# Attention stage of a two-layer streaming encoder: a written order for each engine, first scores among the latent queries, first output halves made in the last tile

## The chip, the cores and the metric

The kernel runs on one core of a Trainium2 chip. The metric is the device time of one execution in microseconds, the median over runs. An execution takes in both layers and both kinds of requests.

## What is computed

Two layers of an encoder run on 1024 prompt tokens and on 8 samples of 16 tokens (1152 tokens, 9 tiles of 128, or 3 blocks of 384). Cut to what matters:

```python
h = rmsnorm(x, norm_g) * (1.0 + scale[:, None]) + shift[:, None]     # shift, scale, gate = silu(c) @ w_mod + b_mod
z = h @ w_in                                # split into conv, latent-attention, local-attention parts
cq = rmsnorm(m_q, q_norm_g); qm = cq @ w_uq # 4 heads: 128 without, 64 with rotary position
kv = ckv_all @ w_ukv                        # keys and values from a latent of 128
s = (einsum(q_nope, k_nope) + einsum(q_rope, k_rope)) * MLA_SCALE    # chunk-causal mask, chunks of 64
p = softmax(s); o_mla = einsum(p, v)        # samples also attend to a cache of 512 keys each
out = concatenate([out_conv, out_mla, out_swa]) @ w_out
x = x + gate[:, None] * out                 # after the second layer a final rmsnorm
```

Everything is float32. Large products are made of three products of float32r parts: hi x hi, lo x hi and hi x lo, where hi is a value rounded on ScalarE and lo is the rest, subtracted on VectorE.

## The kernel before

Each engine has an instruction stream of its own, executed in order; semaphores tie them together. A layer is: the input projection in 22 column chunks, with the local attention tiles spread between the last of them; the latent attention stage; the output projection (`first_out`, `out_a`, `out_b`, lines 997 to 1033). The change concerns the middle part and its two edges.

**Queries.** TensorE makes six rope products (`q_rope`, line 1184, banks 0 to 3) and twelve latent products (`q_latent`, line 1193, a head's weights folded with the key weights, banks 4 to 7), each of 384 columns. ScalarE rotates a rope product by four copies (`turn_query`, line 1530) and copies the even latent ones (`latent_query`, line 1535); VectorE finishes the ropes (`rope_query`, line 1957) and copies the odd latent ones (line 1963). In the old order all of them come before the first scores: scores wait for every rope (`roped`) and every latent copy (`all_latent_queries`, line 1216).

**Groups, jobs, units.** `plan_attention` (line 104) lays out 12 groups: prompt tiles in the order 2, 0, 1, 3, 4, 5, 6, 7 and four pairs of samples between the later ones. A prompt tile has 4 score jobs (one a head, 36 jobs with the samples') and one unit for each key tile (44 units). A job goes: `scores` on TensorE into a bank, or two from tile 4 on (`banks_of`); `maxima` on VectorE (line 1990); `exps` on ScalarE (line 1548); `normalise` on VectorE (line 1996). A unit goes: `turn_probs` on TensorE (line 1268, transposes into bank 4 or 5), a copy to SBUF (even units ScalarE, line 1613, odd ones VectorE), `weigh` on TensorE (line 1287, accumulates in bank 6). After a group: `out` on ScalarE (line 1556), `up_values` on TensorE (line 1310, bank 7), `gate_mla` on VectorE (line 2002), which leaves a tile of `mix`, the input of the output projection. From tile 3 on scores are made of hi and lo parts: `split_keys` (line 1573) once, `split_q` (line 1580) and `stack_q` (line 1592) for each tile, on ScalarE and VectorE.

**Other work in the stage.** Four rows of this layer's gate modulation and, in the first layer, eight of the next layer's are computed from w_mod (`modulation`, line 949, bank 7; copied by VectorE; turned by TensorE, L1346; copied again). SyncE loads w_mod rows, sample caches and w_out blocks of 256 columns into two slots of `raw`, in an order sorted by where the steps stand (`when`, `todo`).

**The order.** `plan_steps` (line 174) writes one list for all engines by rules: scores up to a group ahead, each unit turned one ahead of its weighing. Each engine walks the same list, `STEPS`, and does its own share of each step:

```python
for j in range(GROUPS[1]["jobs"][-1] + 1):
    scores()
    exps(j)
    norms(j - 1)
```

**The edge to the output projection.** After the list, ScalarE makes six pieces of `h_hi` (three blocks by two halves of the 8 rows, line 1630) and VectorE six of `h_lo` (`lo`, line 1763; the last tile's gate between the first and the second). Then both split w_out columns 2 to 5 (ScalarE L1441, VectorE L1811). TensorE's `first_out` makes column blocks 0 and 1 for token blocks 0 and 1, half by half, and `out_a(2)` follows once `residual_a(0)` (line 2066) has read the first. The splits of w_out columns 0 and 1 stand in the last tile, behind the turnings of its units 4 and 6 of 8. SyncE loads the residual `x` (two transfers of 2.3 MB) once the first piece of `h_hi` is made (line 753 to 755). `probs` has 9 slots; `slot_of` (line 143) gives a tile's four jobs slots (2, 3, 6, 7) or (4, 5, 0, 1) in turn; slots 0 to 5 share memory with `h_hi`.

Of the kernel before, what the change touches and what calls it, by code (L numbers as in the profile page):

```python
# [103 lines left out]
def plan_attention():  # L104
# [28 lines left out]
MOD_AT = {(0, 1): 0, (2, 1): 1, (3, 1): 2, (3, 3): 3, (5, 1): 4, (5, 3): 5, (7, 1): 6, (7, 3): 7, (7, 5): 8,  # L133
          (9, 1): 9, (9, 3): 10, (9, 5): 11}
INDEX = {key: gi for gi, key in enumerate(ORDER)}
SPLIT_AT = {1: 3, 2: 4, INDEX["s", 0]: 5, INDEX["s", 1]: 6, INDEX["s", 2]: 7}
NEXT_P = {gi: min((i for i in range(gi + 1, len(ORDER)) if ORDER[i][0] == "p"), default=None) for gi in range(len(ORDER))}
# [36 lines left out]
def plan_steps():  # L174

    steps, done, row = [], {"exp": -1, "norm": -1, "turn": -1, "scores": -1}, None

    def put(what, i):
        steps.append((what, i))
        if what in done:
            done[what] = i

    def exps(upto):
        while done["exp"] < min(upto, done["scores"]):
            j = done["exp"] + 1  # L190
            if SLOT_FREE[j] is not None and SLOT_FREE[j] > done["turn"]:
                return
            put("exp", j)

    def norms(upto):
        while done["norm"] < min(upto, done["exp"]):
            put("norm", done["norm"] + 1)

    def stack(t):
        if ("stack_q", t) not in steps:  # L200
            put("stack_q", t)

    def scores():
        g = GROUP_OF[done["scores"] + 1]
        if g["kind"] == "mla_p" and g["idx"] >= SPLIT_FROM:
            stack(g["idx"])
        put("scores", done["scores"] + 1)
        put("maxima", done["scores"])

    def may_score():  # L210
        j = done["scores"] + 1
        return j < NJOBS and (BANKS_FREE[j] is None or BANKS_FREE[j] <= done["exp"])

    def turn(n):
        if done["turn"] < n:
            put("turn", n)
            put("copy", n)

    for j in range(GROUPS[1]["jobs"][-1] + 1):
        scores()  # L220
        exps(j)
        norms(j - 1)
    norms(GROUPS[0]["jobs"][-1])
    for gi, g in enumerate(GROUPS):
        units = g["units"]
        to = NEXT_P[gi]
        ahead = NJOBS - 1 if to in (None, LAST) else GROUPS[to]["jobs"][-1] + (ORDER[to + 1][0] == "p")
        js = range(done["scores"] + 1, ahead + 1)
        at = [max(len(units) - 1, 1) * i // len(js) for i in range(len(js))]
        if gi in SPLIT_AT:  # L230
            put("split_q", SPLIT_AT[gi])
        if gi == 2:
            put("samples", 0)
        for q, n in enumerate(units):
            for _ in range(at.count(q)):
                exps(done["scores"])
                if may_score():
                    scores()
            if (gi, q) in MOD_AT:
                put("mod", MOD_AT[gi, q])  # L240
                row = MOD_AT[gi, q]
            turn(n)
            if (gi, q) == (0, 1):
                put("split_keys", 0)
            if n < units[-1]:
                turn(n + 1)
            elif gi < LAST and done["exp"] >= GROUPS[gi + 1]["jobs"][-1]:
                norms(GROUPS[gi + 1]["jobs"][-1])
                turn(n + 1)
            if q == 0 and gi - 1 in UP_OF:  # L250
                put("up", gi - 1)
            put("weigh", n)
            if n == units[-1]:
                put("out", gi)
            if q == 0 and gi in SPLIT_AT:
                stack(SPLIT_AT[gi])
            if row is not None and ((gi, q) not in MOD_AT or n == units[-1]):
                put("modT", row)
                row = None
            before = done["exp"]  # L260
            exps(done["scores"])
            norms(before)
            if gi == LAST and q in (3, 5):
                put("split", NIN + q // 4)
        while done["scores"] < ahead:
            exps(done["scores"])
            assert may_score()
            scores()
        if gi < LAST:
            exps(GROUPS[gi + 1]["jobs"][-1])  # L270
            norms(GROUPS[gi + 1]["jobs"][-1])
    return steps


STEPS = plan_steps()
# [30 lines left out]
def build(nc, io):  # L306
# [61 lines left out]
    probs_s = at("probs_s", SPL_AT + 12288, [P, 640])  # L368
# [231 lines left out]

    def p_view(j):
        return probs(j)[:, 0:job_width(j)]

    local_s = psum[:, 6:8, 0:2 * P]
    local_t = psum[:, 6:8, 2 * P:4 * P]
    local_v = psum[:, 6, 2 * P:4 * P]

    with nc.Block() as block:
# [235 lines left out]
        def _(pe):  # L844
# [100 lines left out]
            def layer(L, last):  # L945
# [51 lines left out]
                def first_out():  # L997
# [3 lines left out]
                    for n in range(2):  # L1001
                        for half in range(2):
                            pe.wait_ge(lo_h.sem, lo_h.at(lane.layer, 2 + 2 * n + half + 1))
                            for s in range(2):
                                mm = products(s, [(n, 3 * s + n)], HALF_K[half])
                                if n == 1 and half == 1:
                                    mm.then_inc(z_done.sem, 1)
# [1212 lines left out]
```

## Time and profile before

| | |
|---|---|
| median of 3 runs | 1353.84 us (1346.69 to 1364.53) |
| the profiled execution | 1350.68 us, its span 1348.9 us |
| mean granted TensorE clock | 0.952 |
| TensorE busy | 1249.6 us (93%) |
| VectorE busy | 612.6 us (45%) |
| ScalarE busy | 415.0 us (31%) |
| GpSimd busy | 63.2 us (5%) |
| first layer: first query product, steady output products | 373.45 us, 611.25 us |
| second layer: the same | 1020.6 us, 1241.83 us |

Times in rows are microseconds from the start of the span. PE is TensorE (PEld its weight loads), DVE VectorE, ACT ScalarE, POOL GpSimd, SP SyncE. PEclk is the clock that was granted to TensorE: 1.00 is 2.4 GHz, 0.50 is 1.2 GHz. In a view of stretches a line gives start and end, length, then the busy time (and number of instructions) of PE, PEld, DVE, ACT and POOL, PEclk, the DMA share and GB/s. A wait is idle time of an engine, put down to the work whose end released it.

### The profile page before, as it was taken

What the parts mean: (1) busy time and instruction counts of PE and PEld (TensorE: products, weight loads), DVE (VectorE), ACT (ScalarE), POOL (GpSimd) and SP (SyncE); (2) the same over time, 40 slices, a digit from 0 to 9 for tenths busy, and PEclk for the clock granted to TensorE, in tenths of its full rate; (3) what the DMA queues carried; (4) which work ended last, traced back from release to release, by engine and by line L of the source; (5) the groups of instructions that cost most, each with busy time, mean ns of one, the idle gap of its engine ahead of it and who ended that gap; (6) DMA issues with size and microseconds to landing.
All of it is one profiled execution on the core that took longest, in us unless ns stands there. A gap on an engine that the chain in (4) does not pass through costs nothing.

```text
span 1348.9 us, 18240 instructions
## 1 busy us (share of the span) xinstructions
PE 1249.6 (93%) x7420; PEld 1086.0 (81%) x7420; DVE 612.6 (45%) x1064; ACT 415.0 (31%) x775; POOL 63.2 (5%) x51
## 2 busy tenths in 40 slices
PE   5699999999998899989989999899999889998997
PEld 4599998999955556669989999899996456667996
DVE  3852313346265555553285232233635545555134
ACT  5432311222254234342143232122224334434111
POOL 1100010000000000002120001000000000000211
PEclk9799988999997789999999998999999889998998
DMA  9821211110241135245121112111022203106002
GB/s 349 306 67 31 62 45 32 32 32 28 93 138 42 41 124 164 95 172 181 41 85 55 62 34 73 32 32 32 28 68 99 106 32 102 39 1 240 10 32 110
DMA packets 72063, 112.98 MB, mean 84 GB/s; under 512 B 3617, under 2 KB 55977, under 8 KB 70706
## 3 DMA queue, kind: packets, MB, share of 16 engines
q1 hardware_dynamic: 71986, 111.92, 24.4%
q8 instruction: 52, 0.85, 0.3%
q14 instruction: 25, 0.20, 0.0%
HBM read 94.44 MB, written 16.42 MB: 82 GB/s over the span
## 4 chain that ended last, share of the span: by engine, by line
PE 82%; DVE 10%; ACT 4%; issue 2%; DMA 1%; SPq 1%; DVEq 0%; POOLq 0%; POOL 0%; ACTq 0%
PE psum L964 52%; PE psum L1250 5%; PE psum L1305 4%; PE psum L1284 3%; PE psum L1199 2%; DVE h_lo L1766 2%; DVE h_lo L1775 1%; PE psum L1301 1%; DVE w_lo L1811 1%; PE psum L1190 1%; DMA modw<-in_w_mod 1%; PE psum L955 1%; PE psum L1259 1%; PE psum L1262 1%; DVE scaled L1751 1%
## 5 line engine op out<-in xcount | busy, mean ns | idle before, releaser
L964 PE MATMUL psum<-h_hi,w_hi 128*128 128x384 f32 x1440 | 493.1, 342 | 16.6 <-DVE h_lo L1766 9.5
L964 PE MATMUL psum<-h_lo,w_hi 128*128 128x384 f32 x1440 | 486.3, 338 | 0.0
L964 PE MATMUL psum<-h_hi,w_lo 128*128 128x384 f32 x1440 | 486.0, 337 | 0.0
L964 PEld LDWEIGHTS psum<-h_hi,w_hi 128*128 128x128 f32 x1440 | 274.3, 191 | 23.8 <-issue 18.7
L964 PEld LDWEIGHTS psum<-h_hi,w_lo 128*128 128x128 f32 x1440 | 274.5, 191 | 0.0
L964 PEld LDWEIGHTS psum<-h_lo,w_hi 128*128 128x128 f32 x1440 | 273.9, 190 | 0.0
L1811 DVE TENSOR_TENSOR w_lo<-raw,w_hi 128x1024 fp32r<-128x1024 f32 x62 | 77.1, 1244 | 264.8 <-ACT w_hi L1441 264.3
L1441 ACT ACTIVATE w_hi<-raw 128x1024 fp32r<-128x1024 f32 x62 | 65.7, 1060 | 297.7 <-PE psum L964 216.2
L1993 DVE TENSOR_REDUCE smax<-psum 128x1 f32<-128x640 f32 (+7 forms) x72 | 55.1, 765 | 91.3 <-PE psum L1251 60.7
L1305 PE MATMUL psum<-pT,ckv 128*128 128x512 f32 x144 | 79.2, 634 | 3.3 <-DVE pT L1814 3.3
L1497 ACT ACTIVATE probs_p<-psum,nmax 128x128 f32<-128x128 f32 (+1 forms) x72 | 25.2, 362 | 138.2 <-DVE esink L1811 138.2
L804 POOL TENSOR_TENSOR sq_a<-sq_a,sq_a 128x768 f32<-128x768 f32 x12 | 22.1, 1842 | 894.6 <-ACT sq_a L1395 894.6
L1446 ACT ACTIVATE rot<-psum 32x384 f32<-32x384 f32 (+1 forms) x80 | 59.2, 740 | 8.5 <-DVE svT L1812 5.7
L1553 ACT ACTIVATE probs_lo<-psum,nmax 128x128 f32<-128x128 f32 (+7 forms) x48 | 36.1, 751 | 68.5 <-issue 36.2
L1812 DVE SCALAR_TENSOR_TENSOR x<-psum,mod,x 128x768 f32<-128x768 f32 (+1 forms) x32 | 24.0, 751 | 68.7 <-PE psum L964 67.9
L1613 ACT ACTIVATE pT<-psum 128x512 f32<-128x512 f32 (+1 forms) x44 | 25.0, 568 | 90.8 <-PE psum L1284 47.2
L1812 DVE SCALAR_TENSOR_TENSOR mix<-psum,mix 64x256 f32<-64x256 f32 (+1 forms) x54 | 27.6, 512 | 48.5 <-PE psum L1098 21.1
L1284 PE MATMUL psum<-ident,probs_lo 128*128 128x128 f32 x220 | 40.9, 298 | 8.8 <-DVE probs_hi L1813 5.8
L1284 PEld LDWEIGHTS psum<-ident,probs_lo 128*128 128x128 f32 x220 | 26.1, 149 | 24.9 <-issue 23.5
L1250 PE MATMUL psum<-ckv_hi,qa_hi 128*128 128x512 f32 x72 | 38.6, 537 | 6.3 <-ACT qst L1596 6.3
L1395 ACT ACTIVATE sq_a<-x 128x768 f32<-128x768 f32 x16 | 13.5, 847 | 88.1 <-DVE x L1812 88.1
L1814 DVE COPY pT<-psum 128x512 f32<-128x512 f32 (+1 forms) x44 | 28.8, 655 | 12.9 <-PE psum L1284 10.5
(216 smaller groups left out, 1421.5 us busy)
## 6 DMA issues: line engine op xcount, KB each, us to landing
raw<-in_w_in SPq DMA_DIRECT2D x18, 1024.0 KB, 5.2
raw<-in_w_mod SPq DMA_DIRECT2D x15, 1024.0 KB, 5.1
x<-xT_scratch SPq DMA_DIRECT2D x4, 2304.0 KB, 12.0
modw<-in_w_mod SPq DMA_DIRECT2D x8, 1024.0 KB, 15.0
raw<-in_w_out SPq DMA_DIRECT2D x10, 768.0 KB, 5.4
tab<-in_c_rope SPq DMA_DIRECT2D x6, 1152.0 KB, 5.9
tok<-in_x_prompt SPq DMA_DIRECT2D x2, 2048.0 KB, 10.2
ckvT_c<-in_cache_mla_ckvT SPq DMA_DIRECT2D x8, 512.0 KB, 3.6
```

Of the source, the lines that this page charges most:

```text
L964: mm = pe.matmul(psum[:, bank, 0:BLK], w_[:, k, :], h[:, k, blk(n)], start=(k == 0 and i == 0), stop=(k == KD - 1 and i == 2))
L1199: mm = pe.matmul(psum[:, 4 + m % 4, 0:BLK], mq[:, k, h, :], cq[:, k, blk(n)], start=(k == 0), stop=(k == 1))
L1250: pe.matmul(out[:, a:b], q, k[:, a:b], start=(n == 0), stop=(n == 4 and b < w))
L1284: mm = pe.transpose(out[:, tile(h)], probs(g["jobs"][h])[:, tile(i)], ident[:])
L1305: mm = pe.matmul(psum[:, 6, :], ckv[:, g["keys"][i], :], pT[:, n % 3, :], start=(i == 0), stop=last_one)
L1441: lane.link(act.activation(view(w_hi[w_slot(c)]), src, ACT.Copy), hi_w)
L1446: ins = act.activation(pick(rot[a:a + 32, :]), src[b:b + 32], ACT.Copy)
L1553: lane.link(act.activation(p_view(j), s_view(j), ACT.Exp, bias=nmax[:, s, 0:1], scale=MLA_SCALE, accum_out=psum_p[:, s, 0:1]), expd)
L1811: tt = lambda *a, sig=None: lane.link(dve.tensor_tensor(*a), sig)
L1812: stt = lambda *a, sig=None: lane.link(dve.scalar_tensor_tensor(*a), sig)
L1814: cp = lambda *a, sig=None: lane.link(dve.tensor_copy(*a), sig)
L1993: lane.link(dve.tensor_reduce(smax[:, s, 0:1], s_view(j), AX.X, ALU.max))
```

## The change

1. `plan_steps` and `STEPS` go. Three strings, one for TensorE, ScalarE and VectorE each, give each engine its own order; a letter is a kind of step, and steps of one kind keep their numbers' order. The query products, their rotations and copies are now steps too.
2. TensorE's order begins with ropes 0 to 3 and latents 0 to 6; then scores alternate with the rest: s0, latent 7, s1, rope 4, s2, rope 5, s3, latent 8, s4, latent 9, s5, latent 10, s6, latent 11, s7. Scores need only the latent copies of block 0 and ropes 0 to 3. Ropes 4 and 5 move from banks 0 and 1 into the ring of banks 4 to 7 (`RING`).
3. The split of the keys is two steps; krT's comes first, among the rotations. Query tile 3 is split after the first exponential. The hi and lo keys' and `probs_s`'s places are shifted to allow it.
4. w_mod rows, sample scores, gates and splits stand elsewhere in the stage; in TensorE's order the second w_mod row comes before unit 3 and the value products of groups later by one to five units.
5. The first two pieces of `h_hi` and `h_lo` are halves (block 0, rows 0 to 3) and (block 1, rows 0 to 3); ScalarE and VectorE make them, and the splits of w_out columns 0 and 1, within the last tile: the first half and both splits between the copies of units 34 to 39, the second half at the very end. `slot_of` now gives tiles slots 0 to 3 or 4 to 7, so that the first half's place is free. `first_out` takes the halves in the order of `OUT_HALVES`.
6. SyncE's waits follow: the first sample cache still waits for all latent products, w_mod and w_out loads are sorted by the new places, and `x` is loaded once the last latent output is copied (`ol_c`) and all value products but the last are made.

```diff
@@ def slot_of(j):
     if g["kind"] == "mla_p":
-        return ((2, 3, 6, 7), (4, 5, 0, 1))[side(g["idx"])][i]
+        return HEADS * side(g["idx"]) + i
...
-STEPS = plan_steps()
+RING = [("latent", m) for m in range(2 * HEADS)] + [("rope", 4), ("rope", 5)] + [("latent", m) for m in range(2 * HEADS, 3 * HEADS)]
+OUT_HALVES = ((0, 0), (1, 0), (0, 1), (1, 1), (2, 0), (2, 1))
...
+LETTERS = dict(r="rope", l="latent", s="scores", x="maxima", e="exp", n="norm", t="turn", c="copy", w="weigh", o="out", u="up",
+               m="mod", f="modT", k="keys", q="query", z="stack", b="samples", v="weights", h="half")
+TENSOR_ORDER = (
+    "rrrrlllllllslsrsrslslslslsssstmtwtwfsssmtwstwfsstuwtwmtwfsmtwsstuwtwsstwstuwstuwstwfstwmtwfstwmtwfsm"
+    "twstwfsmtwtwtwftwtuwssmtwstwfstwmtwftwtwsstwtwmtwftuwtwmtwtwtwtwtuwtwftwuw")
+SCALAR_ORDER = (
+    "rrrlrlklleqererelzekelqeeceeceeeoecoeqecozecezeeocqezeceoeceqcezoceeoceeccoeceoecececehocvcvocccho")
+VECTOR_ORDER = (
+    "rrrlrllkxlnxqxrxrxnxnlxnlxkxxnnmcnnxfnxnnnxmcxbxnxnfnncuqxmcfnqxmnxcxnnuxqncxxunnxcunxfncxmqfncxmfnx"
+    "cmnxfnxcmncfcuxnxmncxfnxmcnfcxxcnmnfcuhvcmvccufcuh")
...
-                sp.wait_ge(hi_h.sem, hi_h.at(lane.layer, 3))
+                sp.wait_ge(ol_c.sem, ol_c.at(lane.layer, len(GROUPS)))
+                sp.wait_ge(uv_mm.sem, uv_mm.at(lane.layer, TILES - 1))
...
+                    for i, (n, half) in enumerate(OUT_HALVES[:4]):
+                        pe.wait_ge(lo_h.sem, lo_h.at(lane.layer, 2 + i + 1))
+                        for s in range(2):
+                            if i == 0:
+                                pe.wait_ge(lo_w.sem, lo_w.at(lane.layer, NIN + s - 1))
+                            mm = products(s, [(n, 3 * s + n)], HALF_K[half])
+                            if i == 3:
+                                mm.then_inc(z_done.sem, 1)
+                            if i == s == 0:
+                                up_values(LAST)
...
+                def ring_free(step):
+
+                    what, m = RING[RING.index(step) - 4]
+                    if what == "rope":
+                        pe.wait_ge(roped.sem, roped.at(lane.layer, 4 + m + 1))
+                    else:
+                        copied = (qa_c, qa_v)[m % 2]
+                        pe.wait_ge(copied.sem, copied.at(lane.layer, m // 2 + 1))
...
+                def latent_queries(n):
+
                     for copied in (qa_c, qa_v):
-                        pe.wait_ge(copied.sem, copied.at(lane.layer, HEADS * NBLK // 2))
+                        pe.wait_ge(copied.sem, copied.at(lane.layer, HEADS * n // 2))
...
-                        pe.wait_ge(roped.sem, roped.at(lane.layer, 4 + 2 * NBLK))
+                        pe.wait_ge(roped.sem, roped.at(lane.layer, 4 + 4))
...
-                            all_latent_queries()
+                            latent_queries(1)
...
+                def out_half(i):
+
+                    n, half = OUT_HALVES[i]
+                    if i == 0:
+                        act.wait_ge(score.sem, score.at(lane.layer, NJOBS))
+                        act.wait_ge(pt_T.sem, pt_T.at(lane.layer, GROUPS[INDEX["p", ST - 2]]["units"][-1] + 1))
+                        act.wait_ge(outs.sem, outs.at(lane.layer, 16 * N_STORES))
+                        act.wait_ge(qrs_ok.sem, qrs_ok.at(lane.layer, 1))
+                    elif i == 1:
+                        act.wait_ge(pt_T.sem, pt_T.at(lane.layer, NUNITS))
+                    act.wait_ge(uv_ok.sem, uv_ok.at(lane.layer, (3, 6, TILES)[n]))
+                    ks = slice(4 * half, 4 * half + 4)
+                    lane.link(act.activation(h_hi[:, ks, blk(n)], mix[:, ks, blk(n)], ACT.Copy), hi_h)
...
+                def out_half(i):
+
+                    n, half = OUT_HALVES[i]
+                    if i == 1:
+                        dve.wait_ge(pv.sem, pv.at(lane.layer, NUNITS - 1))
+                    lo(lane, n, half, mix, 2 + i + 1)
```

## Rows read from the trace of the kernel before

**Rows 1.** The page's chain that ended last, shares by engine.
```profile
PE 82%; DVE 10%; ACT 4%; issue 2%; DMA 1%; SPq 1%; DVEq 0%; POOLq 0%; POOL 0%; ACTq 0%
```

**Rows 2.** Stretches, first layer: length, engines' busy time, PEclk, DMA share, GB/s.
```profile
408.20:415.00 6.80, 6.80 (x19) 3.73 (x18) 3.91 (x15) 3.58 (x9) 0.00 (x0) 0.50 0.00 0
425.20:435.50 10.30, 6.02 (x20) 4.55 (x21) 2.88 (x9) 1.78 (x5) 0.00 (x0) 0.50 0.01 2
445.70:462.80 17.10, 14.54 (x57) 7.50 (x58) 5.36 (x15) 3.27 (x7) 0.00 (x0) 0.50 0.19 62
483.30:490.10 6.80, 6.80 (x26) 2.68 (x26) 0.04 (x1) 0.45 (x2) 0.00 (x0) 0.50 0.57 192
490.10:585.20 95.10, 92.06 (x581) 61.29 (x581) 53.54 (x104) 34.32 (x66) 0.00 (x0) 1.00 0.32 104
```

**Rows 3.** The same view, second layer, the first low stretch.
```profile
1056.70:1063.60 6.90, 6.90 (x32) 3.21 (x31) 2.85 (x10) 3.40 (x6) 0.00 (x0) 0.51 0.01 2
```

**Rows 4.** TensorE's waits, front of the first layer's stage: total us, times, longest.
```profile
PE psum L1239 <- DVE qa L1814: 0.8, 1, 0.8
...
PE psum L955 <- DVE mix L1812: 4.1, 1, 4.1
PE psum L1250 <- ACT qst L1596: 3.2, 1, 3.2
PE psum L1284 <- DVE probs_hi L1813: 2.9, 1, 2.9
PE psum L1284 <- DVE probs_lo L1813: 1.5, 1, 1.5
```

**Rows 5.** TensorE's waits, middle of the stage and last tile, first layer.
```profile
PE psum L1301 <- DVE pT L1814: 2.1, 1, 2.1
...
PE psum L1305 <- DVE pT L1814: 1.5, 2, 1.3
```

**Rows 6.** Stretches: front; queries; scores of tiles 2, 0, 1, 3, samples; units.
```profile
373.45:458.88 85.43, 72.97 (x273) 40.09 (x271) 47.89 (x115) 35.50 (x81) 0.00 (x0) 0.82 0.25 83
373.61:396.84 23.23, 23.23 (x73) 13.33 (x71) 16.23 (x26) 14.51 (x30) 0.00 (x0) 1.00 0.31 103
397.64:404.86 7.22, 7.22 (x20) 2.70 (x20) 3.30 (x10) 2.02 (x6) 0.00 (x0) 1.00 0.94 325
404.86:407.75 2.89, 2.89 (x16) 2.04 (x15) 2.43 (x9) 1.13 (x4) 0.00 (x0) 1.00 0.24 96
419.21:423.34 4.13, 4.13 (x17) 2.02 (x16) 3.66 (x9) 1.95 (x4) 0.00 (x0) 1.00 0.40 139
437.29:440.27 2.98, 2.98 (x14) 1.91 (x13) 0.99 (x2) 1.77 (x5) 0.00 (x0) 1.00 0.00 0
511.81:514.74 2.93, 2.93 (x20) 0.90 (x19) 0.53 (x1) 0.48 (x3) 0.00 (x0) 1.00 0.58 166
573.56:578.75 5.19, 5.19 (x26) 3.08 (x25) 1.38 (x2) 1.61 (x3) 0.00 (x0) 1.00 0.00 0
```

**Rows 7.** Timeline of TensorE: start, duration; a value product and a w_mod row.
```profile
440.76 1.06 PE L1319 MATMUL psum<-oL,w_uv 128*128 128x128 f32 x8
...
503.44 1.07 PE L955 MATMUL psum<-raw,cT 128*32 128x256 f32 x16
```

**Rows 8.** Tail, first layer: timelines (TensorE, VectorE), a piece of the chain.
```profile
589.42 0.66 PE L964 MATMUL psum<-h_hi,w_hi 128*128 128x384 f32 x1 [4.21 <-DVE h_lo L1766]
...
594.86 8.93 DVE L1766 TENSOR_TENSOR h_lo<-mix,h_hi 128x1536 fp32r<-128x1536 f32 x5
605.04 5.01 DVE L1811 TENSOR_TENSOR w_lo<-raw,w_hi 128x1024 fp32r<-128x1024 f32 x4 [1.25 <-ACT w_hi L1441]
...
611.25 54.35 PE psum L964 x312
```

**Rows 9.** DMA issues: count, KB each, median us to landing.
```profile
raw<-in_w_out SPq DMA_DIRECT2D x10, 768.0 KB, 5.4
```

**Rows 10.** The same view, the residual's load.
```profile
x<-xT_scratch SPq DMA_DIRECT2D x4, 2304.0 KB, 12.0
```

More of the change, by code:

```diff
@@ L171 @@
     SLOT_FREE[_j] = GROUP_OF[_same[-1]]["units"][-1] if _same else None
[L174 to L272, printed above, removed]
@@ new lines, with steps @@
+SCALAR_ORDER = (
[3 more added lines that the diff above has]
+    "cmnxfnxcmncfcuxnxmncxfnxmcnfcxxcnmnfcuhvcmvccufcuh")
+def steps(order, latents, copies):
+    jobs, units, rows, tiles = range(NJOBS), range(NUNITS), range(N_GATE + N_SHIFT_SCALE), range(SPLIT_FROM, ST)
+    todo = dict(rope=range(2 * NBLK), latent=latents, scores=jobs, maxima=jobs, exp=jobs, norm=jobs, turn=units, copy=copies,
+                weigh=units, out=range(len(GROUPS)), up=UP_OF[:-1], mod=rows, modT=rows, keys=range(2), query=tiles,
+                stack=tiles, samples=range(1), weights=range(2), half=range(2))
+    todo = {what: list(which) for what, which in todo.items()}
+    done = [(LETTERS[c], todo[LETTERS[c]].pop(0)) for c in order]
+    assert not any(todo[what] for what, _ in done), todo
+    return done
@@ L602, in p_view, with rope_bank, latent_bank @@
         return probs(j)[:, 0:job_width(j)]
+    def rope_bank(m):
+        return m if m < 4 else 4 + RING.index(("rope", m)) % 4
+    def latent_bank(m):
+        return 4 + RING.index(("latent", m)) % 4
     local_s = psum[:, 6:8, 0:2 * P]
@@ L739, in layer @@
                 sp.dma_start(w_uv[:], io["w_uv"][L]).then_inc(w_uv_in.sem, 16)
[L740 removed]
+                place = {step: n for n, step in enumerate(TENSOR_STEPS)}
+                when = {("gate", r) if r < N_GATE else ("next", r - N_GATE): place["mod", r] for r in range(N_GATE + N_SHIFT_SCALE)}
                 when.update({("uq", 0): -2, ("ukv", 0): -3})
[L742 removed]
+                todo = [(-1, cache, 0), (-0.9, cache, 1)]
+                todo += [(place["weigh", GROUPS[INDEX["s", b - 2]]["units"][-1]], cache, b) for b in range(2, PAIRS_S)]
                 for x_ in [x for x in loads if x[0] in ("gate", "next") or x in (("out", 0), ("out", 1))]:
@@ L1324, in layer @@
                 rows = 0
-                for what, i in STEPS:
-                    if what == "scores":
+                for what, i in TENSOR_STEPS:
+                    if what == "rope":
+                        q_rope(i)
+                    elif what == "latent":
+                        q_latent(i)
+                    elif what == "scores":
                         scores(i)
@@ L1607, in layer @@
                         exps(i)
-                    elif what == "copy" and COPIER[i] == 0:
+                    elif what == "copy":
                         act.wait_ge(pt_T.sem, pt_T.at(lane.layer, i + 1))
@@ L2025, in layer @@
                         normalise(i)
-                    elif what == "split":
-                        split_w(i)
-                    elif what == "copy" and COPIER[i] == 1:
+                    elif what == "weights":
+                        split_w(NIN + i)
+                    elif what == "half":
+                        out_half(i)
+                    elif what == "copy":
                         dve.wait_ge(pt_T.sem, pt_T.at(lane.layer, i + 1))
```

173 lines of the change are left out of this document (74 added, 99 removed).

## Prediction

> **What bounds the kernel now.** I read the chain of waits first: TensorE holds four fifths of it, VectorE a tenth [rows 1]. So a faster order pays only where TensorE stands still or runs at half clock. The attention stage lies, per layer, between the query products (from 373.45 us in the first layer, 1020.5 in the second) and the steady output pass (from 611.25 and 1241.83). I then took the stage in stretches of one clock level. In the first layer the granted clock is 0.50, that is 1.2 GHz in place of 2.4, in four stretches in which TensorE is busy 6.8, 6.0, 14.5 and 6.8 us [rows 2]; in the second in three, busy 6.9, 7.3 and 5.2 us, of which the first stands [rows 3]. Half of each is what the low level costs: 17.1 and 9.7, together 26.8 us. Then TensorE's waits: at the front of the stage 0.8, 4.1, 3.2, 2.9 and 1.5 us, sum 12.5 [rows 4], and the same five in the second layer, 12.3. In the middle the largest is 2.1 [rows 5]; it is the first of four entries that sum to 3.8, and the second layer has five that sum to 4.5. Twice per layer (together 1.5 us [rows 5]) TensorE waits for a VectorE copy of the last tile, queued behind a w_out split: 2.9 in all. Last, the tail: TensorE is idle 4.21 us before the first output product at 589.42, and the third column block begins only at 611.25, when VectorE's splits, done at 610.05, and its first residual are behind it [rows 8].
>
> **The front of the stage, part by part.** No product is added or taken away; the steps are reordered, so I add up TensorE's work at full clock and ask whether ScalarE and VectorE keep up. The set compared is everything up to the weighing of unit 5 with sample job 16: 18 query products of 1.29 (23.2) [rows 6]; scores of tile 2 7.2, of tile 0 3.9 (four of 2.89/3), of tile 1 5.5 (four of 4.13/3), of tile 3 6.0 (four of 2.98/2), sample job 2.9 [rows 6]; seven turnings and six weighings, 5.19/4 = 1.30 a pair, 8.2 [rows 6]; two w_mod rows of 1.07 with their small turning products (estimated 0.3 each), 2.7; one value product of 1.06 that overlaps the next, 0.9 [rows 7]. Sum, with 0.1 for rounding, 60.5. Before, the same set takes 85.4 us from 373.45 [rows 6], less one value product that now comes later: 84.5. The difference is 24.0 us, and 22.1 in the second layer, where the same view gives 83.55. It is the front waits plus the half-rate cost up to there, so I don't count it again.
>
> Does anything else stop TensorE? In the old stretch VectorE is busy 47.9 us and ScalarE 35.5 [rows 6], nearly the work that must now fit beside 60.5: room, but not much on VectorE. So I walked the three new orders by hand with these durations. The first scores need the four copies of block 0 and rope 3: VectorE's copy of latent 3 ends at about 387.0, TensorE comes at 387.5. From there the score jobs 0 to 7 alternate with latent products, so that the chain scores, maximum, exponential, normalisation runs beside products of 1.29 us; turning of unit 0 comes at 411.9 and its probabilities are ready at 406.7. The split of the keys and of query tile 3, for whose stacking TensorE waited 3.2 us, lies on ScalarE between two exponentials and is done at 409.7, used at 417.7. The second modulation row no longer stands behind a gate of VectorE that stands behind sample queries: that was the 4.1. In this walk no instruction of TensorE up to unit 5 is late; the tightest are the copy of unit 1 (0.4 us), the copy of latent 3 (0.5) and the stacking of tile 4 (1.0). The banks: ropes 4 and 5 move into the ring of banks 4 to 7, and each ring wait (four entries back) is met 0.5 us or more early.
>
> On SyncE, the gate load behind w_uqr is issued some 10 us later (rope 5 ends at 397, not 386) and the first sample cache too (last latent at 406.8, not 396.8). SyncE's queue is in order, so the third row load waits behind them, but its row is used 20 us later. A weight load lands in some 5.4 us [rows 9]; I cost this at nothing; without the cover it would be those 10 us once per layer.
>
> **The clock.** Of the 26.8 us at half rate, how much goes? Bounds: 0 and 26.8. The first low stretch of each layer begins with only 0.8 us of waiting before it, in the small products of tile 0 [rows 2, 4]; the others follow waits of 1.5 to 4.1. From 490 to 585 the clock stays at 1.00 with waits below 1.3 [rows 2, 5]. I take that two stretches of the size of the first remain in each layer: 4 x 3.4 = 13.6 us, between the bounds because those small products stay. The Trainium skill, page "TensorE: Matmul & The Clock Gate", section "A second HAM failure mode: psum-queue depth-cycling", says that frequent short idling between groups of matmuls that cycle PSUM banks lets the clock swing to the lower level. By that the new order, which cycles banks more, would keep all 26.8. The first low stretch agrees with it, the 95 us from 490 on don't; it is rival A.
>
> **The middle.** The new orders keep scores two banks apart and one exponential ahead. The walk up to the sixth modulation row found none of the old waits (8.3 us in both layers). One new wait: the first w_out split now stands in ScalarE's queue ahead of the copy of unit 36. Its block is loaded after modulation row 10 and lands 5.4 us after its last issue [rows 9], with about 1.5 us of issuing before (estimate), 7 in all, while TensorE wants that copy some 7 us after the row; behind ScalarE's split and the copy itself it waits 0 to 3, I take 2, in the first layer only (the last one loads w_out long before).
>
> **The tail.** Before, TensorE's last weighing ends at 589.42 - 4.21 = 585.2, the steady output products start at 611.25: 26.0 us [rows 8]. VectorE sets that: gate, five h_lo (8.93), 1.25 for ScalarE's first w_hi, four w_lo (5.01), 1.2 for the residual and its signal [rows 8]. Now two of the six h_hi and h_lo are made in the last tile, and the products of halves (0,0) and (1,0), 4.2 us each, need nothing new. From the end of the last weighing: 12 products 2.1, values 0.9, gate done at 3.8; four h_lo 7.2 to 11.0; w_hi 12.2; w_lo 17.2; residual and its signal 18.4. TensorE alone: 96 products of 54.35/312 = 0.174 [rows 8] and the values, 17.6; so VectorE still ends last, by 0.8. Gain 26.0 - 18.4 = 7.6, I keep 7.7 with the gate's old wait, 15.4 in both layers. The residual load x, 2.3 MB, lands 12.0 us after its issue [rows 10]; it is issued once the last latent output is copied, 0.7 after the weighing, so at 12.7, and is used at 17.4: hidden by 4.7. The first half's h_lo and the two w_out splits take 1.8 + 2.5 of VectorE between units 35 and 40, where per two units (2.6 us) it has one copy; that is what buys back the 2.9. The value product of the last sample pair moves behind unit 42, the same 0.9 elsewhere.
>
> **Sum.** Waits at the front 24.8, half rate 26.8, middle 8.3, last tile 2.9, tail 15.4: 78.2 us at most. Given back: clock 13.6, the w_out wait 2, and small waits that a walk misses, 3 per layer (bounds 0 and the 24.8 of before, nearer to the tight places found), 6. Net 56.6. The profiled execution took 1350.7 us; less 56.6 is 1294.1. The median of the runs shown is 3.2 above it, so **1297**.
>
> **Rivals.** A: the clock stays as it was. For: the low stretch that no wait explains. Against: 490 to 585. It costs the other 13.2: 1310. B: the front is bound by VectorE's or ScalarE's queue; the new orders place splits and rotations ahead of copies, and 47.9 us beside 60.5 leaves 12. Then the old front waits come back elsewhere, 24.8, and with them the low clock, 13.2: 1335. C: the halves made early save nothing, as the last gate and VectorE's chain start as late as before or x lands late: 15.4 + 2.9 lost, 1315. D, slower than before: in each unit the copy of the turned probabilities stands behind an exponential or a normalisation on its in-order engine, and TensorE waits for it. There are 88 units; from 57/88 = 0.65 us each the gain is gone, over 2% slower from 0.95. With work as long as a w_lo split (1.25 [rows 8]) ahead of every copy it is 1297 + 110 = 1407. Against: before, only a handful of units waited for copies, the longest 2.1 [rows 5], and ScalarE was busy 35.5 of 85 us.
>
> **How the numbers follow.** Forecast 0.70, A 0.12, B 0.08, C 0.06, D 0.04. A change of 2% is 27 us, about what a measurement of this kernel can tell from none: faster means below 1327. Forecast, A and C are faster, 0.88; B is within, 0.08; D slower, 0.04. The range: below, the whole 78.2 would give 1276, and I stop at 1278; above, A and C are in and half of B's distance, 1325.
>
> **What would show it.** Right: no wait of TensorE over 1 us between the first score and unit 5, unit 5 weighed near 434 us in the first layer; the first output product within 0.5 us of the last weighing; the steady output products 18.4 us after it; fewer than 30 us of granted clock 0.5 in both stages together. Wrong: score jobs waiting for an exponential, copies late behind splits, a w_out split waiting for its load over 3 us, or low clock with no wait before it.

## The result, and the profile after

The changed kernel takes 1276.2 us (median of 4 runs, 1275.85 to 1277.6), the one before 1353.65 (median of 4). The ratio is 0.942, 95% interval 0.936 to 0.949: faster by 77 us, where 57 were forecast. The profiled span went from 1348.9 to 1274.3 us, 74.6 less, and the mean granted clock from 0.952 to 0.975.

The page of the kernel after, its chain by engine, answers to [rows 1]:

```profile
PE 88%; DVE 7%; ACT 2%; DMA 2%; SPq 1%; issue 1%; DVEq 0%; POOLq 0%; POOL 0%; ACTq 0%
```

TensorE holds 88% of a shorter chain, VectorE and ScalarE have lost five points between them. The stretches of the stage, for TensorE alone (start and end, length, busy time and instructions, PEclk, DMA share, GB/s), to be held against [rows 2, 3]:

```profile
373.76:434.63 60.87, 60.87 (x266) 1.00 0.36 117
434.63:541.10 106.47, 103.89 (x696) 1.00 0.37 119
541.10:544.50 3.40, 3.40 (x10) 0.52 0.71 230
983.32:1148.61 165.29, 164.30 (x858) 1.00 0.24 79
```

The first line is the set of work that the prediction added up: up to the weighing of unit 5, without one us of idle time and at full clock. Of the granted clock at 0.50, which lay in nine pieces of 75 us in all in the two stages and their tails before, one piece of 3.4 us is left, in the first layer, and none in the second. The waits say why it is there. TensorE's waits in the first layer from 460 to 572 us, in place of [rows 5], and its timeline around the wait:

```profile
PE psum L1253 <- ACT oL_s L1512: 2.6, 1, 2.6
```
```profile
540.32 1.21 PE L1253 MATMUL psum<-pT,ckv 128*128 128x512 f32 x2 [2.58 <-ACT oL_s L1512]
541.32 0.63 PE L1232 MATMUL psum<-ident,probs_lo 128*128 128x128 f32 x2
```

The turning that takes 0.63 us at 541.32 takes 0.38 at 545.55, at full clock again. What TensorE waited for is seen on ScalarE's timeline:

```profile
536.98 1.06 ACT L1393 ACTIVATE w_hi<-raw 128x1024 fp32r<-128x1024 f32 x1 [4.15 <-DMA raw<-in_w_out]
538.07 0.60 ACT L1578 ACTIVATE pT<-psum 128x512 f32<-128x512 f32 x1
538.70 1.06 ACT L1393 ACTIVATE w_hi<-raw 128x1024 fp32r<-128x1024 f32 x1
539.79 0.48 ACT L1512 ACTIVATE oL_s<-psum 128x64 f32<-128x64 f32 x2
```

ScalarE stands 4.15 us in front of its split of w_out column block 0, which has not landed, and the copy of unit 36 and the outputs of the last sample pair (`oL_s`) are queued behind it. TensorE's next weighing writes the bank that those outputs are read from. The copy of unit 36 is done at 538.67, 1.0 us after TensorE has begun to wait; the other 1.6 us are the second split and the outputs behind it. In the second layer that wait is not there; the waits of its stage, up to the last weighing, sum to 1.0 us.

The tail, TensorE's and VectorE's timelines and a piece of the chain, to be held against [rows 8]:

```profile
552.92 1.02 PE L1253 MATMUL psum<-pT,ckv 128*128 128x512 f32 x2
553.38 0.74 PE L903 MATMUL psum<-h_hi,w_hi 128*128 128x384 f32 x1
```
```profile
557.76 7.14 DVE L1726 TENSOR_TENSOR h_lo<-mix,h_hi 128x1536 fp32r<-128x1536 f32 x4
566.14 5.00 DVE L1771 TENSOR_TENSOR w_lo<-raw,w_hi 128x1024 fp32r<-128x1024 f32 x4 [1.25 <-ACT w_hi L1393]
571.18 1.02 DVE L1772 SCALAR_TENSOR_TENSOR x<-psum,mod,x 128x768 f32<-128x768 f32 x1
```
```profile
572.35 54.32 PE psum L903 x312
```

The last weighing ends at 553.94, the first output product overlaps its end (before: 4.21 us idle), and the steady products start at 572.35, 18.4 us after it. In the second layer they start at 1167.02, the last weighing ends at 1148.61: 18.4 again.

**Where the 74.6 us are.** From the first query product to the steady output products the first layer took 611.25 - 373.61 = 237.6 us and takes 572.35 - 373.76 = 198.6; the second took 1241.83 - 1020.62 = 221.2 and takes 1167.02 - 983.32 = 183.7. That is 39.0 and 37.5. All else together became 1.9 longer. Nearly all of that is one more stretch at half rate, in the output pass of the first layer, right behind 24 products of a single column each (sums of squares for the next norm). It costs 1.7 us, and no wait stands before it:

```profile
626.50 2.73 PE L793 MATMUL psum<-ones,sq_a 128*128 128x1 f32 x24
629.10 0.42 PE L903 MATMUL psum<-h_hi,w_hi 128*128 128x384 f32 x1
```
```profile
629.80:633.20 3.40, 3.40 (x15) 0.53 0.00 0
1223.70:1227.10 3.40, 3.40 (x14) 0.53 0.00 0
```

Every profile has these products in both output passes. The kernel before keeps full clock behind them in the first layer and has such a stretch in the second; the changed kernel has one in both.

### The profile page after: what moved, and what is told of

It reads as the page before. It is cut to its first block, busy times and chain, and to the rows that moved or that the text cites. A ratio compares the mean times of both kernels' runs of the same rounds, so it can differ in the third digit from the quotient of the medians.

```text
span 1274.3 us, 18268 instructions
## 1 busy us (share of the span) xinstructions
PE 1218.7 (96%) x7420; PEld 1071.3 (84%) x7420; DVE 614.1 (48%) x1064; ACT 414.8 (33%) x775; POOL 63.2 (5%) x51
## 4 chain that ended last, share of the span: by engine, by line
PE 88%; DVE 7%; ACT 2%; DMA 2%; SPq 1%; issue 1%; DVEq 0%; POOLq 0%; POOL 0%; ACTq 0%
PE psum L903 55%; PE psum L1198 6%; PE psum L1253 5%; PE psum L1232 3%; PE psum L1151 3%; DVE h_lo L1735 1%; PE psum L1141 1%; PE psum L894 1%; PE psum L1188 1%; DMA modw<-in_w_mod 1%; PE psum L1267 1%; DVE h_lo L1726 1%; DVE w_lo L1771 1%; DVE scaled L1711 1%; PE psum L1187 1%; PE psum L1037 1%
## 5 line engine op out<-in xcount | busy, mean ns | idle before, releaser
L1253 PE MATMUL psum<-pT,ckv 128*128 128x512 f32 x144 | 75.1, 604 | 3.1 <-ACT oL_s L1512 2.8
L1497 ACT ACTIVATE probs_lo<-psum,nmax 128x384 f32<-128x384 f32 (+7 forms) x48 | 35.1, 732 | 52.5 <-DVE nmax L1773 23.1
L1774 DVE COPY pT<-psum 128x512 f32<-128x512 f32 (+1 forms) x44 | 28.8, 655 | 27.8 <-PE psum L1232 20.8
L1232 PE MATMUL psum<-ident,probs_lo 128*128 128x128 f32 x212 | 37.7, 286 | 0.0
L1361 ACT ACTIVATE h_hi<-scaled,mod 128x384 fp32r<-128x384 f32 (+1 forms) x48 | 23.9, 570 | 35.5 <-DVE scaled L1711 35.4
```

The costliest lines, as they stand in the source:

```text
L1232: mm = pe.transpose(out[:, tile(h)], probs(g["jobs"][h])[:, tile(i)], ident[:])
L1253: mm = pe.matmul(psum[:, 6, :], ckv[:, g["keys"][i], :], pT[:, n % 3, :], start=(i == 0), stop=last_one)
L1497: lane.link(act.activation(p_view(j), s_view(j), ACT.Exp, bias=nmax[:, s, 0:1], scale=MLA_SCALE, accum_out=psum_p[:, s, 0:1]), expd)
L1774: cp = lambda *a, sig=None: lane.link(dve.tensor_copy(*a), sig)
```

## The experiments

Two numbers help to read them: the span times the mean granted clock, called the time at full clock here, and the rest of the span, called the cost of the low level. They count every microsecond at the low level as half lost, also those in which TensorE is idle. Over the 13 runs that stand beside the first four experiments the kernel before has 1284.2 and 69.9 us, the changed one over its 4 runs 1243.4 and 31.2: by this count 41 us are waits and queues, 39 the clock (means; by the medians it is 77 together). By TensorE's busy time the clock's share is smaller: in the profile of the kernel before it was busy in 61.5 of the 75 us of low clock in the stages and tails, now in 3.4 of 3.4, so 30.8 - 1.7 = 29 of the 76.5 us there are the clock, the other 47 waits and queues. The letters in the diffs are the steps of the orders as the change defines them.

**The old orders in the new form.** All three sequences, the halves and the w_out splits where they stood before; the other edits stay (banks, slots, places, SyncE's waits, the order of halves).

```diff
 TENSOR_ORDER = (
-    "rrrrlllllllslsrsrslslslslsssstmtwtwfsssmtwstwfsstuwtwmtwfsmtwsstuwtwsstwstuwstuwstwfstwmtwfstwmtwfsm"
-    "twstwfsmtwtwtwftwtuwssmtwstwfstwmtwftwtwsstwtwmtwftuwtwmtwtwtwtwtuwtwftwuw")
+    "rrrrllllllllrrllllsssssssssssttwmtwtwfsssstuwssstuwmtwfsstuwssmtwstwfmtwftuwtwsstwsmtwstwfsmtwtwftuwtw"
+    "stwsmtwstwfsmtwstwfmtwftuwtwstwsmtwstwfsmtwstwfmtwtwftuwtwtuwtwtwtwtwtwtww")
...
```

> The changed file with the old sequence of steps written as the three strings: all query products first, splits and both early halves where they were (halves after the last unit). Theory 1 (the whole gain is waits and half-rate clock that the new sequence removes): near the kernel before, 1345 to 1353, less at most the 0.8 us wait per layer, with the low stretches of the clock back. Theory 2 (part of the gain comes from the other edits: ring of banks, weaker waits for queries, slots, the residual's load): at least 8 us below the kernel before, under 1345.

Measured 1346.6 (10 runs), ratio 0.993 (0.990 to 0.997): theory 1, the orders carry all but 7 us. At full clock it takes 1282.5, 2 below the kernel before; the low level costs 62.3 in place of 69.9. Its waits in the stages are the old ones within 0.2 us, but the one of 1.8 before the steady output products is 0.9 now, in both layers, which is the 2 us at full clock. The low clock has the old pattern, in eight pieces of 65 us in all where nine of 75 were. The first three:

```profile
410.40:417.30 6.90, 6.90 (x31) 0.51 0.00 0
427.50:437.70 10.20, 7.14 (x21) 0.51 0.01 2
448.00:454.80 6.80, 4.93 (x25) 0.51 0.47 151
```

The fourth piece of [rows 2] is missing, though the wait in front of it is not: TensorE waits 2.14 us before 482.02 in the kernel before, with the low clock from 483.3 on, and the same 2.14 before 479.47 here, with the clock at 1.00. So most of the 7 us are clock that fell otherwise; whether the other edits or chance made it fall so is not shown.

**The new orders with the old tail.**

```diff
 SCALAR_ORDER = (
-    "rrrlrlklleqererelzekelqeeceeceeeoecoeqecozecezeeocqezeceoeceqcezoceeoceeccoeceoecececehocvcvocccho")
+    "rrrlrlklleqererelzekelqeeceeceeeoecoeqecozecezeeocqezeceoeceqcezoceeoceeccoeceoecececeoccoccvcvohh")
 VECTOR_ORDER = (
...
-    "cmnxfnxcmncfcuxnxmncxfnxmcnfcxxcnmnfcuhvcmvccufcuh")
+    "cmnxfnxcmncfcuxnxmncxfnxmcnfcxxcnmnfcumccvcvufcuhh")
```

> New orders, but both early halves after the last unit and the w_out splits in their old places of the last tile. Theory 1 (VectorE's chain sets the tail): 7.6 us per layer and the 1.45 us waits return, less the wait for w_out (2.6) and its low clock (1.7) that go: 1276 + 18.1 - 4.3 = 1290, plus half-rate clock if the idle time before the first output product brings it back (up to 1.7 per layer). Theory 2 (rival C, the tail ends as late as before anyway): 1272 to 1277.

Measured 1287.6 (4 runs), ratio 0.950 (0.945 to 0.956): 11.4 above the changed kernel, nearly all of it at full clock (1254.5 against 1243.4). That is theory 1, though 2.4 below its 1290 and more below what the low clock in the tails would add to it. Against the version below that has the new tail without the wait for w_out (1270.8) it is 16.8. The 4.2 us before the first output product are back in both layers, with a wait of 2.5 for a gate of VectorE in the first, and with them the low clock lies in the tails: 550.0 to 553.4 and 556.9 to 563.7 us in the first layer, 1161.0 to 1164.4 in the second.

**The new tail alone**, under the old orders of front and middle, with both w_out splits behind the copies of units 36 and 38.

```diff
 SCALAR_ORDER = (
-    "rrrlrlllrrlleeeeeeeeckkceoqeeezcoeqeezecoeeeceecoqzcoeeceeceoqczoceeceeceoqczoceeceececococcvcvohh")
+    "rrrlrlllrrlleeeeeeeeckkceoqeeezcoeqeezecoeeeceecoqzcoeeceeceoqczoceeceeceoqczoceeceececohcovcvccho")
 VECTOR_ORDER = (
...
-    "mcnxfnxmcnxfnmcfnqucxxmcnxfnxmcnxfnmcnfcucucvcvchh")
+    "mcnxfnxmcnxfnmcfnqucxxmcnxfnxmcnxfnmcnfcuhcuvcvcch")
```

> Old sequence up to the last tile, new tail (early halves, splits behind the copies of units 36 and 38). Theory 1 (the parts add up): e1 less 18, that is 1328 to 1335. Theory 2 (the tail's gain needs the front's full clock): e1 less 10 or smaller.

Measured 1327.7 (4 runs), ratio 0.979 (0.973 to 0.985): 18.9 below the old orders in the new form. The waits of the front are the old ones to a tenth, and the low clock lies there at the same places, 10.2, 10.2 and 6.8 us in each layer; the two pieces in the tails are gone with the waits there. So the tail is worth 18.9 us under the old orders and 16.8 under the new ones, and the new orders of front and middle are worth 1346.6 - 1287.6 = 59.0 under the old tail.

**The w_out splits behind the copies.** The one wait that the change brought in, taken away: each split goes behind the copy and the output that it held up.

```diff
 SCALAR_ORDER = (
-    "rrrlrlklleqererelzekelqeeceeceeeoecoeqecozecezeeocqezeceoeceqcezoceeoceeccoeceoecececehocvcvocccho")
+    "rrrlrlklleqererelzekelqeeceeceeeoecoeqecozecezeeocqezeceoeceqcezoceeoceeccoeceoecececehoccovcvccho")
 VECTOR_ORDER = (
...
-    "cmnxfnxcmncfcuxnxmncxfnxmcnfcxxcnmnfcuhvcmvccufcuh")
+    "cmnxfnxcmncfcuxnxmncxfnxmcnfcxxcnmnfcuhmcvcvcufcuh")
```

> The changed kernel with the two w_out splits moved behind the copies of units 36 and 38 and behind the copy of the last sample output. Theory 1 (the 2.6 us wait at unit 36 comes from ScalarE standing at the w_out load, and the clock fell because of it): 2.6 + 1.7 us less, 1272. Theory 2 (TensorE then waits for a later copy or split instead): 1275 or more.

Measured 1270.8 (4 runs), ratio 0.938 (0.933 to 0.943), 5.4 below the changed kernel: 2.6 for the wait, 1.7 for the 3.4 us at half rate behind it, and one us that is within what the low clock outside the stage makes from run to run. Its ScalarE timeline and the stretch from the first query product on:

```profile
536.83 0.48 ACT L1512 ACTIVATE oL_s<-psum 128x64 f32<-128x64 f32 x2 [1.15 <-PE psum L1249]
537.72 1.06 ACT L1393 ACTIVATE w_hi<-raw 128x1024 fp32r<-128x1024 f32 x1 [0.42 <-DMA raw<-in_w_out]
```
```profile
373.76:554.00 180.24, 180.24 (x1048) 1.00 0.38 123
```

The outputs come first now; the split waits 0.42 us for the same load. TensorE is busy for every one of 180 us. This version is the yardstick for the experiments on the clock. It was run once more on another chip and took 1272.4 there (4 runs), so what stands below against 1270.8 is good to some 1.6 us. Its two profiles also differ: behind the 24 products of one column neither output pass has a low stretch in the first profile, and both have one in the second (3.4 us each, 1.7 us dear).

**What brings the low clock.** The prediction had kept 13.6 us of it and the chip kept 1.7, so this is the step to settle. Theory W: waits of TensorE. Theory S: the run of small score products, with or without a wait. First all query products ahead of all scores again, the rest as in the yardstick:

```diff
 TENSOR_ORDER = (
-    "rrrrlllllllslsrsrslslslslsssstmtwtwfsssmtwstwfsstuwtwmtwfsmtwsstuwtwsstwstuwstuwstwfstwmtwfstwmtwfsm"
+    "rrrrllllllllrrllllssssssssssstmtwtwfsssmtwstwfsstuwtwmtwfsmtwsstuwtwsstwstuwstuwstwfstwmtwfstwmtwfsm"
 SCALAR_ORDER = (
-    "rrrlrlklleqererelzekelqeeceeceeeoecoeqecozecezeeocqezeceoeceqcezoceeoceeccoeceoecececehoccovcvccho")
+    "rrrlrlkllrrlleqeeezekeqeeceeceeeoecoeqecozecezeeocqezeceoeceqcezoceeoceeccoeceoecececehoccovcvccho")
 VECTOR_ORDER = (
-    "rrrlrllkxlnxqxrxrxnxnlxnlxkxxnnmcnnxfnxnnnxmcxbxnxnfnncuqxmcfnqxmnxcxnnuxqncxxunnxcunxfncxmqfncxmfnx"
+    "rrrlrllklrlrlxnxqxxxnxnxnxkxxnnmcnnxfnxnnnxmcxbxnxnfnncuqxmcfnqxmnxcxnnuxqncxxunnxcunxfncxmqfncxmfnx"
```

> The version with the splits behind (1270.8, no half-rate stretch in a stage) with all twelve latent and six rope products ahead of the first score on every engine, as before; all else keeps its new order. Nothing has to wait for anything new that I can find. Theory W (waits of TensorE bring the low clock): no wait, so no half-rate stretch, 1270.8 within 1.5. Theory S (a run of small score products with nothing dense among them brings it, wait or no wait): a stretch at 0.50 of 6.8 to 10.2 us near 408 us and near 1040 us, 3.4 to 5.1 us each, so 1277.6 to 1281.0.

Then the same with the old wait in front of the first score:

```diff
-                            latent_queries(1)
+                            latent_queries(NBLK)
```

> As the kernel with all latent products first, and the first score waits for all of them to be read, as in the kernel before. Both theories: a wait of about 0.8 us before the first score in each layer, 1.6 us. Theory W: the wait brings the low clock there, 3.4 to 10.2 us at 0.50 per layer, so 1276 to 1283, against 1270.8 for the run without the wait. Theory S: the same half-rate stretches as in the run without the wait, and only 1.6 us more than it, 1279 to 1283.

Measured 1279.4 and 1282.5 (4 runs each). Both lie in the range of theory S, but not by its way: it had a stretch in each layer of both, and there is one in each run. The same instructions keep full clock in one layer and lose it in the other, and which layer it is differs. First the run without the old wait, then the one with it, each time the stretch of the first and of the second layer:

```profile
409.70:423.30 13.60, 13.60 (x46) 0.51 0.04 5
1018.00:1032.00 14.00, 13.69 (x76) 1.00 0.33 119
```
```profile
409.70:423.30 13.60, 13.29 (x71) 1.00 0.25 79
1016.50:1030.20 13.70, 13.70 (x47) 0.51 0.04 5
```

The prices come out within the 1.6 us between chips: 8.6 above the yardstick is 6.8 for the 13.6 us at half rate and 1.6 for a wait of 0.8 in each layer that I had overlooked (latent 10 takes the bank of rope 4, which VectorE has not finished); the second run adds its two waits of 0.8, and 1.5 us that I can't name. But because of the overlooked wait, which ends at 398.07, 11.6 us before the fall, the run without the old one didn't tell W from S. So a third, in which the last two rope products come before the last two latents, and nothing waits:

```diff
-RING = [("latent", m) for m in range(2 * HEADS)] + [("rope", 4), ("rope", 5)] + [("latent", m) for m in range(2 * HEADS, 3 * HEADS)]
+RING = [("latent", m) for m in range(10)] + [("rope", 4), ("rope", 5), ("latent", 10), ("latent", 11)]
 TENSOR_ORDER = (
-    "rrrrlllllllslsrsrslslslslsssstmtwtwfsssmtwstwfsstuwtwmtwfsmtwsstuwtwsstwstuwstuwstwfstwmtwfstwmtwfsm"
+    "rrrrllllllllllrrllssssssssssstmtwtwfsssmtwstwfsstuwtwmtwfsmtwsstuwtwsstwstuwstuwstwfstwmtwfstwmtwfsm"
...
```

> All latent and rope products ahead of the first score, as in the run e6, but with the two rope products of the last block given out before the last two latents' banks come round, so that nothing waits for VectorE's rope: no wait of TensorE in the front at all. Theory S (the run of small score products is enough by itself): a stretch at 0.50 of 6.8 to 13.6 us behind 408 us in at least one layer, so 3.4 to 6.8 us above the version with the splits behind, run beside it. Theory W (it takes a wait, if only the 0.8 us that e6 had): no such stretch, within 1.5 us of the version with the splits behind.

Measured 1281.6 (4 runs) beside 1272.4 (4 runs) for the yardstick on the same chip: 9.1 above it, more than theory S gave (3.4 to 6.8), as both layers fall. Half of the busy time of the two stretches below is 11.9; the 3.4 us that the yardstick's profile loses in its output passes, and this one's doesn't, go against it. All waits of the front up to 420 us, and the low stretches of both layers:

```profile
PE psum L1187 <- ACT probs_lo L1497: 0.5, 3, 0.2
```
```profile
409.50:419.70 10.20, 10.02 (x38) 0.51 0.02 4
1017.00:1030.70 13.70, 13.70 (x46) 0.51 0.05 14
```

Three waits, the longest 0.2 us, and the clock falls in both layers: S, for this place. How busy TensorE was before the fall in the first layer, in this run and then in the one with all query products first:

```profile
400.00:409.50 9.50, 9.18 (x37) 1.00 0.62 240
```
```profile
400.00:409.40 9.40, 9.40 (x34) 1.00 0.82 279
```

What runs there just before it falls are four jobs of tile 2 (384 columns) and three or four of tile 0 (128 columns), one after another. The first of tile 0 on TensorE's timeline, in the second layer:

```profile
1013.80 0.49 PE L1187 MATMUL psum<-ckvT,qa 128*128 128x128 f32 x2
1014.22 0.49 PE L1188 MATMUL psum<-krT,qr 64*128 64x128 f32 x2
1014.63 0.20 PE L1199 MATMUL psum<-masks 1*128 1x64 bf16 x1
```

In the yardstick the same products stand between latent products of 384 columns and the clock stays. The front up to unit 5 keeps 1.00 in all twelve layers of the six profiles that alternate and have no wait put in; with the scores in a run it falls in four layers of six. So a run of them makes the fall likely, not certain. What in them matters (128 columns, 64 rows, the single row of the mask) was not tried. The 24 products of one column in the output passes have a fall behind them in some profiles and not in others too; whether that is the same thing isn't shown.

**A wait alone**, in the dense surroundings that the new order has: VectorE makes the low half of the latent keys late, and the first split score waits for it.

```diff
 VECTOR_ORDER = (
-    "rrrlrllkxlnxqxrxrxnxnlxnlxkxxnnmcnnxfnxnnnxmcxbxnxnfnncuqxmcfnqxmnxcxnnuxqncxxunnxcunxfncxmqfncxmfnx"
+    "rrrlrllkxlnxqxrxrxnxnlxnlxxxnnmcnnxfnxnnnkxmcxbxnxnfnncuqxmcfnqxmnxcxnnuxqncxxunnxcunxfncxmqfncxmfnx"
```

> The version with the splits behind, with the low half of the latent keys made behind the maxima of job 11 and the norms of jobs 9 to 11 on VectorE: the first split score (job 12) then waits for about 4.1 us in each layer, at 418.5 to 422.6 us in the first. The wait alone: 8.2 us, 1279.0. Theory W: the wait is followed by a stretch at 0.50, 3.4 to 6.8 us long and 1.7 to 3.4 us dear, so 1282.4 to 1285.8. Theory S: no low stretch, since the products around are as dense as they were, 1279.0.

Measured 1284.9 (4 runs), 14.1 above the yardstick. TensorE's timeline and the low stretches:

```profile
418.46 0.20 PE L1199 MATMUL psum<-masks 1*128 1x64 bf16 x1
422.63 0.77 PE L1198 MATMUL psum<-ckv_hi,qa_hi 128*128 128x512 f32 x1 [3.97 <-issue]
423.20 0.63 PE L1198 MATMUL psum<-ckv_lo,qa_hi 128*128 128x512 f32 x1
```
```profile
422.30:429.10 6.80, 6.47 (x28) 0.51 0.01 2
1036.70:1043.50 6.80, 6.52 (x28) 0.51 0.00 0
```

Two waits of 4.0, each with 6.8 us at half rate from its end on: 7.9 and half of 6.47 and of 6.52, 14.4. ("issue" here is VectorE's result, which the profile could not name.) W holds as well, in its place. So the first low stretch of the front comes from the run of small products, and a wait of 4 us brings one by itself, as the 2.6 of the changed kernel did for 3.4 us; the waits of 0.9 for `x` in both tails of the changed kernel brought none. Between them it is open: of four waits of 2.1, in the two layers of the kernel before and of the first experiment, one had a low stretch behind it.

**A smaller thing in the tail.** On top of the yardstick VectorE makes the first residual before its last w_out split.

```diff
-                for c in range(NIN + 2, NIN + 6):
+                for c in range(NIN + 2, NIN + 5):
                     split_w(c)
...
                     residual_a(k)
+                    if k == 0:
+                        split_w(NIN + 5)
```

> The splits of the first two w_out tiles stay behind the copies of units 36 and 38, and VectorE makes the first residual before its last w_out split. That takes away the 0.9 us for which the next stage's first matmul waits for x in each layer. If that wait is on the path: 0.9 x 2 = 1.8 us below the version with the splits behind alone (1270.8), so 1269.0. If the wait only moves to the next residual, no change: 1270.8.

> The version with the splits behind once more, on the chip of the two others of this call, as their yardstick: 1270.8 as before, give or take 1.5.

> The version with the splits behind and the first residual ahead of the last split once more: 1.8 us below its yardstick of this call if the waits of 0.9 us for x were on the path, the same time if they were not. The last call left 1.0 us between them, on two chips.

Measured 1269.8 (6 runs); on one chip 1269.3 (6 runs) beside 1272.4 (4 runs) for its yardstick. The wait of 0.9 is gone from the profile in both layers. The difference is 3.2, but both kernels spread over 4 to 6 us there (1268.95 to 1273.24 and 1267.92 to 1273.67), so between 0 and the expected 1.8 nothing is decided. With the splits behind and this, the kernel runs at 0.9365 of the one before (0.931 to 0.942), and lies 6 to 7 us below the changed one, which was measured on another chip.

**What no run takes apart.** Of the 59 us of the new orders in front and middle, the alternation of scores and query products is worth about 9 (8.6 and 9.1 above). The rest comes with the other moves (the split of the keys and of query tile 3, w_mod rows, sample scores, gates). Their waits are seen in the old profile and gone in the new one, but no run moves one of them alone.

## Why the prediction was right and where it failed

**What was right.** Faster was given 0.88. The largest terms were worked out from what TensorE has to do, and they came out: the front set 60.5 predicted, 60.9 measured; unit 5 weighed near 434, measured 433.6; unit 0 turned at 411.9, measured 411.97; the tail 18.4, measured 18.4 in both layers; the first output product right behind the last weighing. The wait for w_out was put at 0 to 3, taken as 2, in the first layer only, and was 2.6 there; that is in part luck, since the way named, behind the first split and unit 36's copy, accounts for 1.0 of it, and the second split and the outputs behind it were not in the sum. Rivals B, C and D didn't come about, and A neither: no front wait came back, the tail costs 16.8 us when it is put back, and no unit's copy holds TensorE up for more than 0.3 us; the one late step is the output behind unit 36's copy. All four signs of being right came. So did one of being wrong, a w_out split waiting for its load over 3 us (4.15), and, outside the stages, low clock with no wait before it (629.8 and 1223.7 us).

**What failed.** The forecast was 1297, the measurement 1276.2, below the range's lower end of 1278. The step is the first term of "given back": "I take that two stretches of the size of the first remain in each layer: 4 x 3.4 = 13.6 us". One stretch remained in the stages, in which TensorE was busy 3.4 us: 1.7. That is 11.9 of the difference. The reading behind it, that "those small products stay", took the wrong thing as the cause. The products do stay; their run does not. The new order puts a query product between every two of the first eight jobs, and the last experiments show that this keeps the clock: put back in a run they bring the fall without a wait, in most layers. The stretches behind the waits of 1.5 to 4.1 us went with the waits, and the wait put in by hand shows it from the other side.

The second term is "small waits that a walk misses", 6. They were 1.0, all in the second layer: 5.0 more. The w_out wait cost 0.6 more than taken. Net 56.6 + 11.9 + 5.0 - 0.6 = 72.9, and the two stages gained 76.5. The rest of 3.6 lies in no single term; the stretches of low clock in the tails, which the 26.8 did not count, cost half of their busy time, 3.9, part of which the tail's term holds already. The kernel before, TensorE in these two and over all nine low stretches:

```profile
589.10:592.50 3.40, 3.08 (x10) 0.51 0.88 362
...
1217.20:1224.00 6.80, 4.72 (x16) 0.51 1.03 397
sum 75.00, PE 61.50; mean PE 6.83
```

From the stages to the forecast: 18.0 of the 20.8 us by which it was too high are these terms, less the 1.9 that all else became longer (11.9 + 5.0 - 0.6 + 3.6 - 1.9). The other 3 are the step from the profiled execution to the median: the kernel before has its median 3.2 above the execution that was profiled, and the prediction carried this over; the changed kernel has it 0.1 above (1276.2, 1276.13).

**The range.** "below, the whole 78.2 would give 1276, and I stop at 1278". The terms for the clock and for small waits each had a lower bound of zero, stated beside it, and the range cut them off. That the outcome is 1276 to the microsecond is chance, though: the stages gained 76.5, not 78.2, and the 1.9 lost elsewhere and the 3 from the median happen to make up for it.

**The rule weighed there.** The Trainium skill, page "TensorE: Matmul & The Clock Gate", section "A second HAM failure mode: psum-queue depth-cycling", tells of a kernel that cycles PSUM banks and whose TensorE idles briefly and often between groups of matmuls, so that its clock swings between the two levels. The prediction made of it that more cycling alone would keep the low clock (rival A, 1310), and that step failed. In the version with the splits behind, scores and query products alternate between two sets of banks, TensorE was busy for all of the 180 us shown, and the clock stayed full. So the trace does not contradict what the Trainium skill says: the short idling that it names was not there. Nor does such idling account for the first low stretch: TensorE was busy 9.40 of 9.40 us before it in the run with all query products first.

## What to carry to other kernels

When TensorE is to keep its clock, look for two things in the trace, not one: its waits of some us, and stretches in which it is busy but with a run of small products. Dense products that are ready anyway (here the later blocks' query products) were worth about 9 us more as filling between the small ones than in a block ahead of them. And a step that waits for a load belongs behind whatever its in-order engine owes the bounding engine, even where the load is expected in time: here it cost 2.6 us and 1.7 behind it.

## What was unexpected of the hardware

The clock went to 1.2 GHz though TensorE had been busy 9.18 of the 9.5 us before, in another run 9.40 of 9.40, and in two copies of the same instructions, one a layer, it fell in one and not in the other. It also fell behind 24 products of one column each: in one profile of a kernel in both layers, in another profile of the same kernel in neither. A wait of 4.0 us cost 3.3 us more than itself, in both layers; the waits of 0.9 cost only themselves. And the kernel before spreads over 1346 to 1366 us (one run of 6740 us left out) at an almost constant time at full clock (1279 to 1287 us): its spread is the clock's.
